# Rotary embedding of q and k in a decoder-trunk kernel: exchanging a head's halves by SBUF-to-SBUF transfers in place of a permutation product

## Chip, cores and metric

One core of one Trainium2 chip runs the whole kernel in one launch. The metric is the device time of that launch in microseconds, the median of several executions. TensorE is called PE in the profile, VectorE DVE, ScalarE ACT, GpSimd POOL and SyncE SP.

## What is computed

Two layers of a hybrid decoder trunk for 512 prompt tokens and 8 decode tokens, 520 columns in all. Each layer projects the normalised input to four mixers and their gates. The part that matters here is the attention's q and k, eight query heads and two key heads of 64 channels:

```python
def rope(x, pos):
    half = HEAD_DIM // 2
    ...
    x1, x2 = xf[..., :half], xf[..., half:]
    return jnp.concatenate([x1 * cos - x2 * sin, x2 * cos + x1 * sin], axis=-1).astype(x.dtype)

q = rope(rms_norm(aq.reshape(B, L, N_HEADS, HEAD_DIM), q_norm), pos)
k = rope(rms_norm(ak.reshape(B, L, N_KV_HEADS, HEAD_DIM), k_norm), pos)
```

Beside it runs mixer B, a depthwise convolution of width 31 over 512 channels (4 chunks of 128). Attention, the other mixers, the merge and a SwiGLU follow.

## The kernel before

Channels lie on the 128 partitions and tokens along a row, so everything is a chunk of 128 x 520 numbers. Every dense product is made exact enough by splitting each operand into a rounded part and its rest (`whi`, `wlo` for a weight tile, `xhi`, `xlo` for the input): three products for each of 8 input chunks, each in two halves of 260 columns, so 48 matmuls for an output chunk.

The list `SLOTS` is the order of the mixing stage: **slot** n is output chunk n, and all engines walk that list. Slots 0 to 7 give the wide convolution's inputs, 8 to 11 the four chunks of q (two heads each), 12 k, 13 v, and 14 to 25 the short convolution. In each slot, TensorE does the 48 matmuls (L604) and then its `side(n)`; VectorE does its `side(n)`, the weight rest two slots ahead (L1271, `lo`), the transfer of the chunk out of PSUM times rstd (L1262, `evac`), and some taps of the wide convolution (L1265, the table `TAPS_AT`: four in slots 8 and 9, two in slots 10 to 17); ScalarE does its `side(n)`, the rounding of a weight tile three slots ahead (L967, `hi`), and squares or sigmoids. Weight tiles come from DRAM on SP's queue (L579), two tiles to a load of 1 MB, into a ring of two loads. There are two PSUM buffers for output chunks, so slot n on TensorE needs slot n-2 taken out by VectorE.

GpSimd computes the fourth chunk of the wide convolution beside all this: 30 times a product `ssum <- cfu * weight` (L1728, TENSOR_SCALAR) and an addition `cacc <- cacc + ssum` (L1731, TENSOR_TENSOR), each waiting for the one before.

q and k go through these steps, chunk c = 0 to 4 (four of q, then k). ScalarE squares the chunk; TensorE sums over a head by a product with a block matrix of ones (L637, slot 9+c); ScalarE makes the factor by a logarithm and an exponential, `gt[:, 1]` (L950, slot 10+c); VectorE multiplies the chunk by gain and factor (L1265 `q<-q,pr,gt`, slot 10+c, semaphore `qk_n`); TensorE multiplies the result by the permutation matrix `rot`, which exchanges the two halves of each head and negates one, into PSUM banks 2 and 3 (L648, slot 11+c, `qk_r`); VectorE, in slot 12+c, multiplies those banks by the sine into `gt[:, 2]` (L1262 `gt<-m,cs`, `qk_rot`), the chunk by the cosine (L1262 `q<-q,cs`), and adds the two (L1262 `q<-q,gt`, `qk_out`). For c = 4 the names read `kt` in place of `q`. In slot 17 VectorE copies the decode tokens' columns to `kts` and `qz`, and TensorE's `side(17)` waits for those before its scores (L663).

```python
r1 = tt(halves(gt[:, 2]), m_halves(2), halves(sinm), ALU.mult, "qk_rot")
r2 = tt(v, v, cosm, ALU.mult)
st.need(r1, r2)
tt(v, v, gt[:, 2], ALU.add, "qk_out")
```

Of the kernel before, what the change touches and what calls it, by code (L numbers as in the profile page):

```python
# [27 lines left out]
ALU = mybir.AluOpType  # L28
# [3 lines left out]
P = 128  # L32
# [4 lines left out]
T = SEQ + NS  # L37
TH = T // 2
# [3 lines left out]
HEAD = 64  # L42
GROUP = 4
# [58 lines left out]
S_AQ, S_AV, S_SCH, S_GATE_A, S_GA, S_GATE_B = (FIRST[k] for k in ("aq", "av", "sch", ("gate", 0), "ga", ("gate", 1)))  # L102
# [75 lines left out]
NPAR = _at  # L178
CST = {}
_at = 0  # L180
for _name, _w in (("cos", T), ("sin", T), ("amask", 2 * P), ("ident", P), ("ones", P), ("ones64", P), ("rot", P),
                  ("eye8", NS)):
    CST[_name] = (_at, _at + _w)
    _at += _w
# [3 lines left out]
def constants():  # L188

    c = np.zeros((P, NCST), np.float32)  # L190
    half = HEAD // 2
    inv = np.float32(10000.0) ** (-np.arange(half, dtype=np.float32) / np.float32(half))
    pos = np.concatenate([np.arange(SEQ), np.full(NS, 2048)]).astype(np.float32)
    ang = (pos[:, None] * inv[None, :]).astype(np.float32)
    ang = np.tile(ang.T, (4, 1))
    q = np.arange(P)

    def put(name, v):
        a, b = CST[name]
        c[:v.shape[0], a:b] = v  # L200
    put("cos", np.cos(ang))
    put("sin", np.sin(ang))
    key = np.arange(2 * P)
    put("amask", np.where((key[None, :] > q[:, None]) & (key[None, :] <= q[:, None] + P), 0.0, NEG))
    put("ident", np.eye(P))
    put("ones", np.ones((P, P)))
    put("ones64", (q[:, None] // HEAD == q[None, :] // HEAD).astype(np.float32))
    rot = np.zeros((P, P))
    for m in range(P):
        if m % HEAD < half:  # L210
            rot[m + half, m] = -1.0
        else:
            rot[m - half, m] = 1.0
    put("rot", rot)
    put("eye8", np.eye(NS))
    s, t = q[:, None], q[None, :]
    glam = ((s // CHUNK == t // CHUNK) & (s <= t)).astype(np.uint32)
    tt = np.arange(T)
    scanm = np.tile(((tt % CHUNK != 0) & (tt < SEQ)).astype(np.float32), (P, 1))
    return c, glam, scanm  # L220


def build(nc, wt, xt, gm, par, cst, glam_d, scan_d, kc, vc, scst, ccst, gst,
          yt, o_sc, o_scs, o_cc, o_ccs, o_k, o_ks, o_v, o_vs, o_g, o_gs):
    ctx = ExitStack()
    with ctx:
# [44 lines left out]
        q = place("q", [P, GROUP, T], offset=base)  # L271
        kt = place("kt", [P, T], offset=base + 4 * SL)
# [26 lines left out]
        gt = place("gt", [P, 4, T])  # L299
# [13 lines left out]
        def cst_(name, rows=P):  # L313
            a, b = CST[name]
            return cs[0:rows, a:b]
# [4 lines left out]
        cosm, sinm, ident, ones = cst_("cos"), cst_("sin"), cst_("ident"), cst_("ones")  # L320
# [3 lines left out]
        m4 = ctx.enter_context(nc.psum_tensor("m4", [P, 4, 512], F32))  # L324
# [7 lines left out]
        def halves(ap):  # L332
            return ap.rearrange("p (a n) -> p a n", a=2)

        def m_halves(b):
            return m4[:, b:b + 2, 0:TH]
# [9 lines left out]
        def sem(name):  # L346
# [55 lines left out]
            "qk_ln": "their logarithm: the banks are read",  # L402
            "qk_rn": "the factor",
            "qk_n": "normalised chunk",
            "qk_r": "its rotated half, in banks 2 and 3",
            "qk_rot": "... times the sine: the banks are read",
            "qk_out": "rotated chunk",
            "v_t": "v transposed, in banks 0 and 1",
            "v_copied": "... in SBUF",
# [80 lines left out]
        s = {n: sem(n) for n in signals}  # L490
# [78 lines left out]
        with nc.Fori(0, DEPTH) as layer:  # L569
            with nc.Block() as block:  # L570
# [28 lines left out]
                def _(pe):  # L599
# [22 lines left out]
                    def side(n):  # L622
# [5 lines left out]
                        c = n - (S_AQ + 1)  # L628
                        if 0 <= c < 5:
# [6 lines left out]
                            for h in range(2):  # L636
                                ins = nc.tensor.matmul(m4[:, h, 0:TH], cst_("ones64"), gt[:, 0, h * TH:h * TH + TH],  # L637
                                                       start=True, stop=True)
                            ins.then_inc(s["qk_ss"], 1)
                        c = n - (S_AQ + 3)  # L640
                        if 0 <= c < 5:

                            pe.wait_ge(s["qk_n"], c + 1)
                            if c >= 1:
                                pe.wait_ge(s["qk_rot"], c)
                            src = q[:, c] if c < GROUP else kt[:]
                            for h in range(2):
                                ins = nc.tensor.matmul(m4[:, 2 + h, 0:TH], cst_("rot"), src[:, h * TH:h * TH + TH],  # L648
                                                       start=True, stop=True)
                            ins.then_inc(s["qk_r"], 1)  # L650
                        if n == S_AV + 3:

                            pe.wait_ge(s["acc_out"], S_AV + 1)
# [4 lines left out]
                        if n == SATT:  # L658
# [3 lines left out]
                            for b in range(NS):  # L662
                                ins = nc.tensor.matmul(m4[0:NQ, 0, 0:P], flat(qz)[:, b * NQ:b * NQ + NQ], kts[:, b],  # L663
                                                       start=b == 0, stop=b == NS - 1)
# [6 lines left out]
                        if n == SATT + 3:  # L671
# [3 lines left out]
                            for b in range(NS):  # L675
                                ins = nc.tensor.matmul(m4[:, 3, b * NS:b * NS + NS], vs[:, b], pts[:, b],
                                                       start=True, stop=True)
# [67 lines left out]
                        if n == G_U:  # L745
# [3 lines left out]
                            for c in range(NCHUNK):  # L749
                                r = slice((c % 2) * CHUNK, (c % 2) * CHUNK + CHUNK)  # L750
                                for h in range(4):
# [4 lines left out]
                                        start=True, stop=True)  # L756
# [189 lines left out]
                def _(a):  # L946
# [27 lines left out]
                    def rsqrt(out, in_, scale, eps, first, last):  # L974

                        st.need(act(out, in_, ACT.Ln, first, scale=scale, bias=eps))
                        act(out.rearrange("p a n -> p (a n)"), out.rearrange("p a n -> p (a n)"), ACT.Exp, last,
                            scale=-0.5)
# [17 lines left out]
                    def side(n):  # L996
# [14 lines left out]
                        if 0 <= c < 5:  # L1011
                            a.wait_ge(s["qk_ss"], c + 1)
                            if c:
                                a.wait_ge(s["qk_n"], c)
                            rsqrt(halves(gt[:, 1]), m_halves(0), 1.0 / HEAD, RMS_EPS, "qk_ln", "qk_rn")
                        if n == SATT:
                            a.wait_ge(s["v_t"], 1)
                            act(vb[:].rearrange("p b n -> p (b n)"), m4[:, 0], name="act_order")
                            st.need(act(vnew, m4[0:NS, 1, 0:P], name="v_copied"))
                            a.wait_ge(s["vs_in"], 16)  # L1020
                            for b in range(NS):
                                load(vs[WIN - 1:WIN, b], vnew[b:b + 1], "vnew_in")
# [235 lines left out]
                def _(dve):  # L1258
                    st = Steps(dve, "vec_order")

                    def tt(out, in0, in1, op, name=None):
                        return st(nc.vector.tensor_tensor(out, in0, in1, op), name)  # L1262
# [45 lines left out]
                    def side(n):  # L1308
# [11 lines left out]
                        if 0 <= c < 5:  # L1320

                            v = q[:, c] if c < GROUP else kt[:]
                            dve.wait_ge(s["qk_r"], c + 1)
                            if c:
                                st.need(("qk_out", c))
                            r1 = tt(halves(gt[:, 2]), m_halves(2), halves(sinm), ALU.mult, "qk_rot")
                            r2 = tt(v, v, cosm, ALU.mult)
                            st.need(r1, r2)
                            tt(v, v, gt[:, 2], ALU.add, "qk_out")
# [573 lines left out]
```

## Time and profile before

| | us |
|---|---|
| median of 3 runs (2064.05 to 2064.55) | 2064.53 |
| the profiled execution | 2065.61 |
| its span, first to last instruction | 2063.8 |

| engine | busy us | share of the span |
|---|---|---|
| TensorE matmul | 2012.2 | 97% |
| TensorE weight load | 1971.5 | 96% |
| VectorE | 1226.2 | 59% |
| ScalarE | 781.8 | 38% |
| GpSimd | 380.7 | 18% |

The profile describes one execution, so its rows add up to its own time, which is 1.1 us above the median. Busy TensorE time is modelled from the starts of the matmuls and doesn't tell by itself which engine is waited for; the waits and the timeline of a stretch do. Both layers run the same program, the second one 1024 us after the first. In the rows, "out<-in" are the program's buffers: `m` is the four-bank PSUM tensor `m4`, `acc` the output chunks in PSUM, `cs` the constants (cosine, sine, matrices), `pr` the parameters; all other names are in SBUF.

### The profile page before, as it was taken

The numbers are of one execution on the slowest core, as the hardware profiler recorded it, in microseconds if no ns is written. First come the engines' busy times: TensorE is split into PE (matmuls) and PEld (weight loads), VectorE is DVE, ScalarE is ACT, GpSimd is POOL, SyncE is SP. The second block draws the span as 40 slices with busy tenths as digits, with TensorE's granted clock in tenths as the row PEclk, the third lists the DMA queues.
The fourth block names the chain that finished last, engine by engine and source line by source line (L and its number), as shares of the span: only waits on it lengthen the run. The fifth ranks groups of instructions, "written<-read, shape, count | busy, mean of one in ns | idle before, by whom it ended". The sixth has DMA issues, their size and how long they took to land.

```text
span 2063.8 us, 39007 instructions
## 1 busy us (share of the span) xinstructions
PE 2012.2 (97%) x16572; PEld 1971.5 (96%) x16572; DVE 1226.2 (59%) x1667; ACT 781.8 (38%) x1209; POOL 380.7 (18%) x238
## 2 busy tenths in 40 slices
PE   6999999999999999999989999999999999999998
PEld 6999999999999999999989999999999999999998
DVE  4898668755556543355539985787455454533445
ACT  4323533553543332233233144336534334322332
POOL 0695000311103000000307940002111130000003
PEclk9999999999999999999999999999999999999999
DMA  7524522222322222222444243222223222232223
GB/s 239 98 85 83 83 77 98 83 95 83 124 82 103 82 97 92 97 82 79 141 121 80 101 63 82 93 83 87 91 82 141 86 92 92 82 101 85 99 77 128
DMA packets 70041, 199.57 MB, mean 97 GB/s; under 512 B 41555, under 2 KB 42707, under 8 KB 51409
## 3 DMA queue, kind: packets, MB, share of 16 engines
q1 hardware_dynamic: 26144, 177.50, 26.1%
q10 hardware_dynamic: 43760, 20.11, 5.7%
q8 instruction: 104, 1.70, 0.4%
q14 instruction: 33, 0.26, 0.0%
HBM read 187.42 MB, written 12.29 MB: 97 GB/s over the span
## 4 chain that ended last, share of the span: by engine, by line
PE 42%; DVE 6%; issue 1%; ACT 1%; POOL 0%; ACTq 0%; DVEq 0%; POOLq 0%
PE acc L604 40%; DVE cacc L1265 1%; DVE wlo L1271 1%; DVE q L1262 1%; DVE sct L1265 0%; ACT tmp L950 0%; PE m L701 0%; PE m L688 0%; PE m L714 0%; PE m L618 0%; DVE gt L1262 0%; DVE small L1262 0%; PE m L816 0%; PE m L788 0%; PE m L826 0%
## 5 line engine op out<-in xcount | busy, mean ns | idle before, releaser
L604 PE MATMUL acc<-xhi,wlo 128*128 128x260 f32 x3680 | 754.1, 286 | 28.7 <-PEq L567 19.4
L604 PE MATMUL acc<-xhi,whi 128*128 128x260 f32 x3680 | 743.0, 284 | 0.0
L604 PE MATMUL acc<-xlo,whi 128*128 128x260 f32 x3680 | 742.4, 283 | 0.0
L604 PEld LDWEIGHTS acc<-xhi,wlo 128*128 128x128 f32 x3680 | 571.0, 189 | 42.3 <-issue 34.6
L604 PEld LDWEIGHTS acc<-xhi,whi 128*128 128x128 f32 x3680 | 569.3, 189 | 0.0
L604 PEld LDWEIGHTS acc<-xlo,whi 128*128 128x128 f32 x3680 | 569.0, 189 | 0.0
L1271 DVE TENSOR_TENSOR wlo<-raw,whi 128x1024 fp32r<-128x1024 f32 (+3 forms) x344 | 435.7, 1275 | 36.7 <-ACT whi L967 35.3
L967 ACT ACTIVATE whi<-raw 128x1024 fp32r<-128x1024 f32 (+3 forms) x344 | 332.1, 994 | 252.7 <-PE acc L604 195.2
L950 ACT ACTIVATE gt<-gt 128x520 f32<-128x520 f32 x226 | 144.4, 639 | 214.1 <-DVE gt L1262 209.2
L1262 DVE TENSOR_TENSOR gt<-acc,rstd 128x520 f32<-128x520 f32 x80 | 55.9, 699 | 210.6 <-PE acc L604 185.6
L604 PE MATMUL acc<-hhi,whi 128*128 128x260 f32 x704 | 141.5, 282 | 0.0
L604 PE MATMUL acc<-hlo,whi 128*128 128x260 f32 x704 | 141.5, 282 | 0.0
L604 PE MATMUL acc<-hhi,wlo 128*128 128x260 f32 x704 | 141.4, 282 | 0.0
L1265 DVE SCALAR_TENSOR_TENSOR cacc<-cfu,pr,cacc 128x512 f32<-128x512 f32 x180 | 140.1, 804 | 1.6
L1772 POOL TENSOR_TENSOR tmp<-x 128x520 f32<-128x520 f32 x2 | 2.1, 1054 | 656.0 <-DVE x L1691 656.0
L1728 POOL TENSOR_SCALAR ssum<-cfu,pr 128x512 f32<-128x512 f32 x60 | 120.9, 2016 | 5.9
L1659 DVE TENSOR_TENSOR gt<-acc,rstd 128x520 f32<-128x520 f32 x44 | 30.8, 700 | 134.0 <-PE acc L604 122.8
L604 PEld LDWEIGHTS acc<-hlo,whi 128*128 128x128 f32 x704 | 108.4, 188 | 0.0
L604 PEld LDWEIGHTS acc<-hhi,wlo 128*128 128x128 f32 x704 | 108.3, 188 | 0.0
L604 PEld LDWEIGHTS acc<-hhi,whi 128*128 128x128 f32 x704 | 108.3, 188 | 0.0
L604 PE MATMUL acc<-ohi,wlo 128*128 128x260 f32 x512 | 106.7, 290 | 0.5 <-DVE gt L1262 0.5
L604 PE MATMUL acc<-ohi,whi 128*128 128x260 f32 x512 | 103.0, 283 | 0.0
(224 smaller groups left out, 2093.8 us busy)
## 6 DMA issues: line engine op xcount, KB each, us to landing
raw<-in_wt SPq DMA_DIRECT2D x142, 1024.0 KB, 4.8
raw<-in_wt SPq DMA_DIRECT2D x16, 768.0 KB, 4.3
raw<-in_wt SPq DMA_DIRECT2D x16, 640.0 KB, 3.8
x<-yt ACTq DMA_DIRECT2D x2, 2080.0 KB, 9.4
yt<-x ACTq DMA_DIRECT2D x16, 260.0 KB, 2.1
x<-in_xt SPq DMA_DIRECT2D x4, 520.0 KB, 5.0
yt<-in_xt SPq DMA_DIRECT2D x1, 2080.0 KB, 16.3
s<-in_gs ACTq DMA_DIRECT2D x4, 512.0 KB, 3.8
```

The costliest lines, as they stand in the source:

```text
L604: ins = nc.tensor.matmul(out[:, h], a, b[:, h * TH:h * TH + TH], start=first and n == 0, stop=last and n == 2)
L950: return st(nc.scalar.activation(out, in_, func, **kw), name)
L967: nc.scalar.activation(whi[:, ts, 0:length], raw[:, e, off:off + length], ACT.Copy)\
L1262: return st(nc.vector.tensor_tensor(out, in0, in1, op), name)
L1265: return st(nc.vector.scalar_tensor_tensor(out=out, in0=in0, scalar=scalar, in1=in1, op0=op0, op1=op1), name)
L1271: nc.vector.tensor_tensor(wlo[:, ts, 0:length], raw[:, e, off:off + length], whi[:, ts, 0:length].bitcast(F32), ALU.subtract)\
L1659: nc.vector.tensor_tensor(halves(t), acc_of(0), halves(rstd[:]), ALU.mult)\
L1728: st(nc.gpsimd.tensor_scalar(ssum[:, 0:SEQ], cfu[:, c, w:w + SEQ], par_("cc", c * W2 + w), None, ALU.mult))
L1772: nc.gpsimd.tensor_tensor(tmp[:, 0], x[:, 0], x[:, 0], ALU.mult).then_inc(s["ss_sq"], 1)
```

## The change

The matrix `rot` and TensorE's products with it (L648) are gone. In their place ScalarE, in its `side` of slot 11+c after the logarithm and exponential, waits for `qk_n` c+1 and, from the second chunk on, for `qk_rot` c, and issues four transfers on its own DMA queue, each 32 partitions x 520 numbers from SBUF to SBUF: the halves exchanged, into `gt[:, 3]`. The sign is put into the sine. VectorE waits for the four transfers (16 counts each) and multiplies `gt[:, 3]` by the sine. The constants that are loaded at the start get 128 columns narrower.

```diff
-    put("sin", np.sin(ang))
+    first = (np.arange(P) % HEAD < half)[:, None]
+    put("sin", np.where(first, -np.sin(ang), np.sin(ang)))
...
-                        c = n - (S_AQ + 3)
-                        if 0 <= c < 5:
-
-                            pe.wait_ge(s["qk_n"], c + 1)
-                            if c >= 1:
-                                pe.wait_ge(s["qk_rot"], c)
-                            src = q[:, c] if c < GROUP else kt[:]
-                            for h in range(2):
-                                ins = nc.tensor.matmul(m4[:, 2 + h, 0:TH], cst_("rot"), src[:, h * TH:h * TH + TH],
-                                                       start=True, stop=True)
-                            ins.then_inc(s["qk_r"], 1)
...
+                        c = n - (S_AQ + 3)
+                        if 0 <= c < 5:
+
+                            a.wait_ge(s["qk_n"], c + 1)
+                            if c:
+                                a.wait_ge(s["qk_rot"], c)
+                            for p0 in range(0, P, HEAD // 2):
+                                p1 = p0 ^ (HEAD // 2)
+                                src = q[p1:p1 + HEAD // 2, c] if c < GROUP else kt[p1:p1 + HEAD // 2]
+                                load(gt[p0:p0 + HEAD // 2, 3], src, "qk_r")
...
-                            dve.wait_ge(s["qk_r"], c + 1)
+                            dve.wait_ge(s["qk_r"], 64 * (c + 1))
...
-                            r1 = tt(halves(gt[:, 2]), m_halves(2), halves(sinm), ALU.mult, "qk_rot")
+                            r1 = tt(gt[:, 2], gt[:, 3], sinm, ALU.mult, "qk_rot")
```

ScalarE's program around slot 12 before (`gt<-q` is the square, the next two the factor, `whi` the rounded weight tile; in brackets the semaphores waited for):

```order
L950 ACTIVATE gt<-q 128x520 [waits qk_ss,acc_out]
L950 ACTIVATE gt<-m 128x520 [waits qk_n,qk_ss]
L950 ACTIVATE gt<-gt 128x520 [waits qk_ln]
L967 ACTIVATE whi<-raw 128x1024 [waits acc_done]
L950 ACTIVATE gt<-kt 128x520 [waits qk_ss,acc_out]
```

And now (its lines are numbered 17 lower):

```order
L933 ACTIVATE gt<-q 128x520 [waits qk_ss,acc_out]
L933 ACTIVATE gt<-m 128x520 [waits qk_n,qk_ss]
L933 ACTIVATE gt<-gt 128x520 [waits qk_ln]
L936 DMA gt<-q 32x520 [waits qk_rot,qk_n]
L936 DMA gt<-q 32x520 x3
L950 ACTIVATE whi<-raw 128x1024 [waits acc_done]
L933 ACTIVATE gt<-kt 128x520 [waits qk_ss,acc_out]
```

Four DMA issues and a wait for VectorE's `qk_rot` stand between the factor and the weight tile's rounding.

VectorE's program around slot 13 before:

```order
L1262 TENSOR_TENSOR kt<-acc,rstd 128x520 [waits acc_done]
L1265 SCALAR_TENSOR_TENSOR cacc<-cfu,pr,cacc 128x512 [waits vec_order] x2
L1262 TENSOR_TENSOR gt<-m,cs 128x520 [waits qk_out,qk_r]
L1262 TENSOR_TENSOR q<-q,cs 128x520
L1262 TENSOR_TENSOR q<-q,gt 128x520 [waits vec_order,qk_rot]
```

And now (its lines are numbered 7 lower):

```order
L1255 TENSOR_TENSOR kt<-acc,rstd 128x520 [waits acc_done]
L1258 SCALAR_TENSOR_TENSOR cacc<-cfu,pr,cacc 128x512 [waits vec_order] x2
L1255 TENSOR_TENSOR gt<-gt,cs 128x520 [waits qk_out,qk_r]
L1255 TENSOR_TENSOR q<-q,cs 128x520
L1255 TENSOR_TENSOR q<-q,gt 128x520 [waits vec_order,qk_rot]
```

The number and order of VectorE's instructions is the same; the first input of the product with the sine is `gt` in place of `m`.

## Rows read from the trace of the kernel before

**Rows 1.** The page's first part: engine, busy us, share, instructions.

```profile
PE 2012.2 (97%) x16572; PEld 1971.5 (96%) x16572; DVE 1226.2 (59%) x1667; ACT 781.8 (38%) x1209; POOL 380.7 (18%) x238
```

**Rows 2.** Busy time by stretch, slots 9 to 19 of layer 0 (stretch, length, engines, clock).

```profile
80.00:160.00 80.00, 76.21 (x588) 74.25 (x587) 75.80 (x95) 21.80 (x32) 76.20 (x42) 0.98 0.31 95
```

**Rows 3.** Waits of PE, 93 to 139 us: us in total, times, longest.

```profile
PE m L663 <- DVE qz L1342: 3.6, 1, 3.6
```

**Rows 4.** Timeline of DVE, slots 12 and 13: start us, us, engine, line.

```profile
101.07 0.69 DVE L1262 TENSOR_TENSOR kt<-acc,rstd 128x520 f32<-128x520 f32 x1
101.68 1.40 DVE L1265 SCALAR_TENSOR_TENSOR cacc<-cfu,pr,cacc 128x512 f32<-128x512 f32 x2
103.00 0.69 DVE L1262 TENSOR_TENSOR gt<-m,cs 128x520 f32<-128x520 f32 x1
103.61 1.19 DVE L1262 TENSOR_TENSOR q<-q,cs 128x520 f32<-128x520 f32 x1
104.90 1.00 DVE L1262 TENSOR_TENSOR q<-q,gt 128x520 f32<-128x520 f32 x1
105.83 0.75 DVE L1265 SCALAR_TENSOR_TENSOR q<-q,pr,gt 128x520 f32<-128x520 f32 x1
106.50 2.31 DVE L1271 TENSOR_TENSOR wlo<-raw,whi 128x1024 fp32r<-128x1024 f32 x1
108.73 0.69 DVE L1262 TENSOR_TENSOR vt<-acc,rstd 128x520 f32<-128x520 f32 x1
```

**Rows 5.** Timeline of POOL beside it.

```profile
100.16 2.42 POOL L1728 TENSOR_SCALAR ssum<-cfu,pr 128x512 f32<-128x512 f32 x1
102.66 1.58 POOL L1731 TENSOR_TENSOR cacc<-cacc,ssum 128x512 f32<-128x512 f32 x1
104.34 1.89 POOL L1728 TENSOR_SCALAR ssum<-cfu,pr 128x512 f32<-128x512 f32 x1
106.31 1.41 POOL L1731 TENSOR_TENSOR cacc<-cacc,ssum 128x512 f32<-128x512 f32 x1
```

**Rows 6.** Instructions on gt, 60 to 130 us: duration ns min/median/max, starts.

```profile
L1262 DVE TENSOR_TENSOR gt<-m,cs x5: 685/686/687, 95.3 to 125.1; 128x520 f32<-128x520 f32 x5
L1262 DVE TENSOR_TENSOR cfu<-gt x2: 686/686/687, 63.3 to 69.0; 128x512 f32<-128x512 f32 x2
```

**Rows 7.** All instructions of L1728 and of L1731: duration ns min/median/max.

```profile
L1728 POOL TENSOR_SCALAR ssum<-cfu,pr x60: 1562/1893/2952, 73.4 to 1205.9; 128x512 f32<-128x512 f32 x60
L1731 POOL TENSOR_TENSOR cacc<-cacc,ssum x60: 1265/1496/2301, 75.1 to 1207.5; 128x512 f32<-128x512 f32 x60
```

**Rows 8.** Timeline of PE at the end of slot 12.

```profile
100.33 1.04 PE L637 MATMUL m<-gt,cs 128*128 128x260 f32 x4
101.20 1.04 PE L648 MATMUL m<-q,cs 128*128 128x260 f32 x4
101.89 0.60 PE L604 MATMUL acc<-xhi,wlo 128*128 128x260 f32 x2
```

**Rows 9.** Timelines: ACT's factor and rounding, the first product, DMA issues.

```profile
90.50 0.64 ACT L950 ACTIVATE gt<-gt 128x520 f32<-128x520 f32 x1
91.04 1.04 ACT L967 ACTIVATE whi<-raw 128x1024 fp32r<-128x1024 f32 x1
95.33 0.69 DVE L1262 TENSOR_TENSOR gt<-m,cs 128x520 f32<-128x520 f32 x1
93.66 29.22 SPq L579 DMA_DIRECT2D raw<-in_wt  x3
130.09 5.14 ACTq L953 DMA_DIRECT2D vs<-tmp  x8
```

**Rows 10.** DMA issues: count, KB each, median us from issue to landing.

```profile
raw<-in_wt SPq DMA_DIRECT2D x142, 1024.0 KB, 4.8
vs<-tmp ACTq DMA_DIRECT2D x16, 0.5 KB, 1.7
```

**Rows 11.** Busy time by stretch around the wait of rows 3 (the 0.50 is PE's clock).

```profile
139.00:140.00 1.00, 1.00 (x7) 1.00 (x6) 1.00 (x1) 0.00 (x0) 0.92 (x2) 0.50 0.00 0
```

More of the change, by code:

```diff
@@ L180 @@
 _at = 0
-for _name, _w in (("cos", T), ("sin", T), ("amask", 2 * P), ("ident", P), ("ones", P), ("ones64", P), ("rot", P),
+for _name, _w in (("cos", T), ("sin", T), ("amask", 2 * P), ("ident", P), ("ones", P), ("ones64", P),
                   ("eye8", NS)):
@@ L207, in constants @@
     put("ones64", (q[:, None] // HEAD == q[None, :] // HEAD).astype(np.float32))
[L208 to L214, printed above, removed]
     put("eye8", np.eye(NS))
@@ L404, in build @@
             "qk_n": "normalised chunk",
-            "qk_r": "its rotated half, in banks 2 and 3",
-            "qk_rot": "... times the sine: the banks are read",
+            "qk_r": "its halves exchanged, by DMA",
+            "qk_rot": "... times the sine, which has the sign",
             "qk_out": "rotated chunk",
```

## The prediction
> **What bounds the kernel now.** I read the page first: TensorE is busy for 97% of the span and VectorE for 59% [rows 1], which makes a product taken from TensorE look like time won. That is a mean over stages, so I went to the stretch that the change touches. From 80 to 160 us of layer 0, slots 9 to 19, VectorE is busy for 75.80 of 80 us and GpSimd for 76.20 [rows 2]; both are full there, and TensorE's 76.21 says little, since its busy time is modelled. Next, who waits for whom: between 93 and 139 us VectorE has no wait on another engine at all, and TensorE has one, 3.6 us at the end, when it stands before its scores until VectorE has copied `qz` [rows 3]. So in these slots the chain runs through VectorE, and whatever TensorE loses or gains before that wait is made up in it.
>
> Then VectorE slot by slot. One slot takes 7.66 us (`kt<-acc` at 101.07 to `vt<-acc` at 108.73) with no gap [rows 4]. TensorE's own slot is not much shorter: 48 matmuls, the sum over a head and the product with the permutation, which begins at 101.20 and gives way at 101.89, 0.69 us [rows 8].
>
> What stretches VectorE's slot? The product with the sine from PSUM takes 685 to 687 ns in all five instances [rows 6], though GpSimd is in the middle of something each time. The next one, `q<-q,cs`, has the same size but both inputs in SBUF, and takes 1.19 us [rows 4]; a product of two SBUF inputs before GpSimd has begun took 0.686 (`cfu<-gt`) [rows 6]. Beside GpSimd's starts [rows 5] this reads as a turn-taking. The 0.69 us of work in `q<-q,cs` would begin at 104.11 if it ends at 104.80, and GpSimd's addition ends at 104.24. `wlo<-raw,whi` lasts 2.31 us and ends at 108.81; its own 1.21 us would begin at 107.60, and the addition beside it ends at 107.72. So a VectorE instruction with two SBUF inputs stands until GpSimd's addition is within 0.12 us of its end, and GpSimd in turn stands until VectorE's has let go. The addition that began at 102.66 had to let the tap end at 103.08 and held VectorE off until 104.11, some 1.1 us. GpSimd's product with a weight holds for less: the addition `q<-q,gt` at 104.90 was stretched by 0.31 us to 1.00, hence about 0.5 us after `q<-q,cs` let go, and the pair of taps at 101.68 was not stretched at all (1.40 us for two) though such a product ran until 102.58. In one slot VectorE stands for 0.50 + 0.31 + 1.10 = 1.91 us.
>
> **The change, part by part.**
>
> *Products with the permutation.* Ten chunks in two layers, 0.69 us of TensorE each, up to 0.87 if the change of matrices after it is counted like that after the sum over a head [rows 8]: 6.9 to 8.7 us of TensorE. I cost this at nothing. It lies beside VectorE's slot; TensorE reaches its scores earlier and waits there longer than 3.6 us [rows 3].
>
> *The product with the sine.* Its own length stays 0.69 us, but its first input moves from PSUM to SBUF, and it becomes one of the instructions that take turns with GpSimd. In the slot shown it begins at 103.00, just when GpSimd's addition gets its turn, and that addition did 0.69 of its 1.1 us under it for free. Now VectorE stands: the product would end at 104.80 instead of 103.69, `q<-q,cs` no longer stands behind that addition (0.50 us back), but GpSimd's next product gets in between. Below, it costs nothing, if GpSimd's turns slide under other free work (the 0.69 us of `kt<-acc`, or the part of its product in which it holds nobody off). Above, each of the ten loses 1.11 us, 104.11 less 103.00, and nothing is given back: 11.1 us. I take the middle that follows from GpSimd's work being fixed: it has 30 such pairs a layer whatever VectorE does, and each product takes 0.69 us away in which it ran for free, so 10 x 0.69 = 6.9 us. It is nearest to the row because the addition filled that window wholly.
>
> The Trainium skill (SBUF — State Buffer, section "Who interferes with whom") speaks against the change by a rule of its own: a VectorE instruction with two SBUF inputs contends with a GpSimd instruction that reads SBUF, and whichever starts first keeps the shared port for the whole instruction. The rows agree for GpSimd's addition and not for its product, beside which two taps ran unstretched; by the page the sum would be that of the fourth rival below.
>
> *The transfers.* ScalarE issues eight transfers of 0.5 KB in 5.14 us, 0.64 us each [rows 9], so four cost it 2.6 us a chunk. Its slot holds that beside a weight tile of 1.04 us and three instructions of about the factor's 0.64 [rows 9], in all 5.6 of 7.66 us, so ScalarE keeps up. Behind them on its engine stand the weight tile's rounding, due one VectorE slot later, and the next square, due in the same slot; both come about 2.6 us later and are still early. On its queue nothing else is issued between the convolution's states in slot 8 and slot 17. A small transfer from SBUF to SBUF lands 1.7 us after issue; a load of 1 MB takes 4.8 [rows 10]. From one product with the sine to the next: 0.69 + 2.6 + 1.7 = 5.0 us, under a slot's 7.66, so chunks 1 to 4 are covered by the rest of VectorE's slot, with 2.7 us to spare. Chunk 0 is tight. Its factor is out at 91.14, four issues end at 93.7, landing at about 95.4, and VectorE wants it at 95.33 [rows 9]. A weight load starts at 93.66, so it may land as late as such a load, 4.8 us after issue, at 98.5. Bounds: 0 to 3.2 us a layer; I take 0.5, near the small transfer's row, so 1.0 us in two layers.
>
> *Constants 128 columns narrower, the sign in the sine:* nothing; the load stands before the first slot among loads of several MB.
>
> Sum, against the profiled execution: 2065.6 + 0 + 6.9 + 1.0 = 2073.5. Its time is 1.1 us above the median of the runs, so the forecast is **2072.4 us**, 7.9 us or 0.4% slower. A measurement of this kernel can tell about 0.2%, 4.1 us, from no change.
>
> **The rivals.**
>
> 1. *GpSimd moves aside.* Its turns fall under VectorE's remaining free work, or it ends its 30 pairs earlier and gives later slots back what it took. For: its product holds nobody off for about two thirds of its length. Against: GpSimd is busy for 76.20 of 80 us [rows 2], and in the row its addition uses the whole window. 0 to 3 us: about 2066.5, no change.
> 2. *TensorE was the bound after all,* and what it is spared shows. For: 97% [rows 1], and its slot is within a few tenths of VectorE's. Against: VectorE has no gap and TensorE ends in a wait of 3.6 us. It would decide only if VectorE's stretched instructions hid a wait for TensorE. 6.9 to 8.7 us less: 2056 to 2057.6, faster.
> 3. *The transfers are late.* If they land as slowly as a weight load, 4.8 us, the loop is 0.69 + 2.6 + 4.8 = 8.1 us, 0.4 over VectorE's slot for eight chunks, 3 us, and chunk 0 costs 2.7 us more than I took, in two layers 5. On top of the forecast: 2080. Against: the small transfers run on rings that the weight loads use for less than half of each two slots.
> 4. *GpSimd's product holds for its whole length too.* The product with the sine would then stand behind 1.56 us [rows 7] instead of a part of 1.1: 10 x 1.56 = 15.6 us, 2080. Against: the two taps at 101.68.
> 5. *TensorE's clock.* After its wait of 3.6 us the granted clock was 0.50, 1.2 GHz [rows 11]. Shorter slots on TensorE and longer ones on VectorE leave it waits of about 1.7 us in each of five slots; if these lower the clock too, its 48 matmuls take up to twice 5.8 us and it becomes the bound: some 3 us more than the forecast in each layer if half of that shows, 2078.
>
> **How the numbers follow.** Forecast 0.55, rival 1 0.18, rival 2 0.06, rival 3 0.10, rival 4 0.07, rival 5 0.04. The predicted time is the forecast's. The range runs from 2064.5 (the lower bound, nothing) to 2080.5: the upper bound of 11.1 us and a late chunk 0 (5 us) give 2080.6, and rivals 3 to 5 lie within. Left out are rival 2 and perhaps half of rivals 3 and 4, under 2 in 10. Faster by over 0.2%: rival 2, 0.06. Within 0.2%: rival 1, 0.18. Slower: the rest, 0.76.
>
> **What would show it.** In the changed profile: `gt<-gt,cs` longer than 0.69 us in several instances, up to 1.8, where `gt<-m,cs` was 0.69 in all; VectorE without waits between slots 12 and 17 except one before the first of them, under 1 us; TensorE's wait for `qz` several us longer than 3.6; four issues of 0.6 us a chunk on ScalarE's queue and no VectorE wait for ScalarE's weight tile. A `gt<-gt,cs` of 0.69 throughout with no later time would be rival 1; VectorE waits on the transfers in every chunk, rival 3; TensorE at 0.50 within slots 12 to 16, rival 5. A time under 2060 would make the reading of the bound wrong.

## The result, and the profile after

The changed kernel takes 2070.32 us (median of 9 runs, 2067.47 to 2072.84), the kernel before 2064.55 beside it (9 runs, 2063.89 to 2066.09). The ratio is 1.0028, with a 95% interval of 1.0018 to 1.0038: 5.8 us slower, between 3.7 and 7.8. The forecast was 7.9 us slower. The profiled execution took 2071.61 us, its span 2068.5. Its times are set against those of the profile before in two layers, so a difference in one place stands for two.

The page's first part, after, stands beside [rows 1]:

```profile
PE 2005.3 (97%) x16532; PEld 1965.3 (95%) x16532; DVE 1229.8 (59%) x1667; ACT 781.7 (38%) x1209; POOL 386.2 (19%) x238
```

TensorE lost 40 matmuls and 6.9 us of busy time, and nothing of that shows in the time. VectorE and GpSimd, with the same number of instructions as before, are busy for 3.6 and 5.5 us longer. Where VectorE's go is seen in its timeline of the same slot as [rows 4] (start us, us, engine, line):

```profile
101.99 0.69 DVE L1255 TENSOR_TENSOR kt<-acc,rstd 128x520 f32<-128x520 f32 x1
102.60 1.40 DVE L1258 SCALAR_TENSOR_TENSOR cacc<-cfu,pr,cacc 128x512 f32<-128x512 f32 x2
103.92 1.78 DVE L1255 TENSOR_TENSOR gt<-gt,cs 128x520 f32<-128x520 f32 x1
105.63 0.69 DVE L1255 TENSOR_TENSOR q<-q,cs 128x520 f32<-128x520 f32 x1
106.42 0.92 DVE L1255 TENSOR_TENSOR q<-q,gt 128x520 f32<-128x520 f32 x1
107.26 0.75 DVE L1258 SCALAR_TENSOR_TENSOR q<-q,pr,gt 128x520 f32<-128x520 f32 x1
107.93 2.32 DVE L1264 TENSOR_TENSOR wlo<-raw,whi 128x1024 fp32r<-128x1024 f32 x1
110.17 0.69 DVE L1255 TENSOR_TENSOR vt<-acc,rstd 128x520 f32<-128x520 f32 x1
```

And GpSimd's beside it, to be read with [rows 5]:

```profile
103.58 1.57 POOL L1724 TENSOR_TENSOR cacc<-cacc,ssum 128x512 f32<-128x512 f32 x1
105.24 2.42 POOL L1721 TENSOR_SCALAR ssum<-cfu,pr 128x512 f32<-128x512 f32 x1
107.75 1.42 POOL L1724 TENSOR_TENSOR cacc<-cacc,ssum 128x512 f32<-128x512 f32 x1
```

The slot is 8.18 us long (101.99 to 110.17) where it was 7.66. The product with the sine takes 1.78 us instead of 0.69: with both inputs in SBUF it stands behind the addition that GpSimd began at 103.58. But `q<-q,cs`, which stood 0.50 us behind that addition before, now follows in 0.69, and `q<-q,gt` is 0.08 shorter: 1.09 - 0.50 - 0.08 = 0.51, and 0.52 by the slot's length, within rounding. GpSimd's next product, ready when the addition ended at 105.15, does not get between the two: it takes 2.42 us, where 1.56 is its least [rows 7]. That fits a wait until the second of VectorE's is nearly done: its 1.56 us would begin at 106.10 (107.66 less 1.56), and `q<-q,cs` ends at 106.32.

The instances of the product, 60 to 131 us (duration ns min/median/max, first and last start):

```profile
L1255 DVE TENSOR_TENSOR gt<-gt,cs x5: 687/1783/1784, 95.8 to 127.6; 128x520 f32<-128x520 f32 x5
```

Four of five are long. The fifth, in slot 16, takes 0.69; there `kt<-kt,cs` is the long one, as it was before. TensorE's wait before its scores, 3.6 us in [rows 3], has become (us in total, times, longest):

```profile
PE m L646 <- DVE qz L1335: 9.5, 1, 9.5
```

It gives back what TensorE was spared, and VectorE's delay comes on top. Behind this wait TensorE's granted clock stayed at 0.50 (1.2 GHz) for longer. The next two rows show the same stretch of its work, 3.4 to 5.4 us after its scores began (stretch, its length, PE's busy time, clock, DMA share, GB/s). Before:

```profile
142.00:144.00 2.00, 2.00 (x16) 0.92 0.97 389
```

and after:

```profile
144.46:146.46 2.00, 2.00 (x10) 0.53 0.96 389
```

So TensorE did 10 matmuls there instead of 16, and came later to its next meeting with VectorE, the product with `sprob`. Before, it stood waiting for `sprob`:

```profile
138.61 3.44 PE L663 MATMUL m<-kts,qz 128*64 128x128 f32 x16 [3.59 <-DVE qz L1342]
153.50 0.40 PE L604 MATMUL acc<-xhi,whi 128*128 128x260 f32 x2
154.10 0.27 PE L669 MATMUL m<-cs,sprob 64*128 64x64 f32 x1 [0.20 <-DVE sprob L1357]
```

After, it needed 15.71 us instead of 14.89 from the start of the scores to the last pair of matmuls ahead of that product:

```profile
141.09 3.67 PE L646 MATMUL m<-kts,qz 128*64 128x128 f32 x16 [9.54 <-DVE qz L1335]
156.80 0.40 PE L598 MATMUL acc<-xhi,whi 128*128 128x260 f32 x2
157.28 0.27 PE L652 MATMUL m<-cs,sprob 64*128 64x64 f32 x1
```

The transfers are as cheap as hoped here. The issue of chunk 0's and chunk 1's, the landing, and an issue further on that nobody had asked about, on ScalarE's queue:

```profile
90.92 3.13 ACTq L936 DMA_DIRECT2D gt<-q  x4
97.62 2.44 ACTq L936 DMA_DIRECT2D gt<-q  x4
152.16 1.12 ACTq L936 DMA_DIRECT2D o_v<-vt  x1
```

```profile
gt<-q ACTq DMA_DIRECT2D x32, 65.0 KB, 2.0
```

VectorE has no wait for any of them; the first product begins at 95.75, right behind its predecessor. The last issue, the write of v to memory after the decode tokens' softmax, took 0.37 us in both layers before, 1.12 and 0.93 now. Behind it on ScalarE stands the rounding of branch A's chunk, for which VectorE waited 1.33 us before:

```profile
155.93 0.72 DVE L1255 TENSOR_TENSOR olo<-sct,ohi 128x520 fp32r<-128x520 f32 x1 [2.08 <-ACT ohi L933]
```

So two places lose time. The first is known, VectorE's product. The second, TensorE and ScalarE both late for what follows the scores, was not foreseen.

### The profile page after: what moved, and what is told of

Read it like the earlier page. It is cut to its first block, busy times and chain, and to the rows that moved or that the text cites. A ratio compares the mean times of both kernels' runs of the same rounds, so it can differ in the third digit from the quotient of the medians.

```text
span 2068.5 us, 38967 instructions
## 1 busy us (share of the span) xinstructions
PE 2005.3 (97%) x16532; PEld 1965.3 (95%) x16532; DVE 1229.8 (59%) x1667; ACT 781.7 (38%) x1209; POOL 386.2 (19%) x238
## 4 chain that ended last, share of the span: by engine, by line
PE 43%; DVE 5%; issue 1%; ACT 1%; POOL 0%; DVEq 0%; POOLq 0%
PE acc L598 40%; DVE cacc L1258 1%; DVE wlo L1264 1%; DVE gt L1255 0%; DVE q L1255 0%; ACT tmp L933 0%; PE m L684 0%; PE m L671 0%; PE m L697 0%; PE m L612 0%; DVE sct L1258 0%; PE m L799 0%; PE m L771 0%; PE m L809 0%; PE m L646 0%
```

## The experiments

Two stretches of each profile separate the two places. Stretch A runs from the arrival of k's chunk (`kt<-acc`, slot 12) to the first copy of `qz`; stretch B from ScalarE's `sprob` exponential to its first `prob` one. T is TensorE's part of what leads into B: from the start of its scores to the last pair of matmuls ahead of its product with `sprob`. Between stretches A and B, from the copy of `qz` to `sprob`, 10.75 to 10.79 us passed in every kernel and layer of this table. All values are us, worked out from starts in the timelines, layer 0 / layer 1.

| kernel | A | B | T | issue of `o_v` | time against before (95%) |
|---|---|---|---|---|---|
| before | 37.10 / 37.09 | 16.10 / 16.09 | 14.89 / 14.88 | 0.37 / 0.37 | |
| the change | 38.66 / 38.66 | 16.81 / 16.81 | 15.71 / 15.87 | 1.12 / 0.93 | 1.0028 (1.0018 to 1.0038) |
| e1: product from SBUF alone | 38.69 / 38.69 | 16.32 / 16.19 | 15.61 / 15.51 | 0.37 / 0.37 | 1.0023 (1.0013 to 1.0032) |
| e2: product back in PSUM | 37.09 / 37.09 | 16.09 / 16.92 | 14.79 / 15.38 | 0.37 / 0.61 | 1.0014 (1.0005 to 1.0023) |
| e5: sine in PSUM | 37.08 / 37.10 | 16.09 / 16.93 | 15.19 / 15.12 | 0.37 / 0.62 | 1.0013 (1.0004 to 1.0022) |
| e7: transfers alone, unread | 37.10 / 37.13 | 16.09 / 16.08 | 14.86 / 14.91 | 0.37 / 0.37 | 0.9999 (0.9990 to 1.0008) |
| e9: neither products nor transfers | 37.08 / 37.09 | 16.89 / 16.80 | 15.72 / 15.65 | 1.23 / 0.80 | 1.0011 (1.0001 to 1.0020) |
| e10: products, and transfers waited for | 37.10 / 37.12 | 16.42 / 16.10 | 15.71 / 14.93 | 0.37 / 0.37 | 0.9999 (0.9990 to 1.0008) |

**e1, the product's source alone.** The kernel before, TensorE's product kept, its result unread:

```diff
-                            r1 = tt(halves(gt[:, 2]), m_halves(2), halves(sinm), ALU.mult, "qk_rot")
+                            r1 = tt(gt[:, 2], gt[:, 3], sinm, ALU.mult, "qk_rot")
```

> The kernel before, with one change: VectorE's product with the sine reads gt[:, 3] in SBUF (old contents, so the rotation is left out of q and k) in place of the PSUM banks. TensorE's product with the permutation and all waits stay; there are no transfers. Theory A (the product, with two SBUF inputs, now takes turns with GpSimd): four of five products a layer stretch to about 1.78 us, the copy of qz comes 2.0 us later in each layer, the whole about 4.1 us slower than before, 2068.6. Theory B (the transfers and their issue on ScalarE cost the time): no change from before, within 1 us, and all products at 0.69 us.

Measured: 2068.07 us, ratio 1.0023. The instances of the product, 60 to 131 us:

```profile
L1262 DVE TENSOR_TENSOR gt<-gt,cs x5: 689/1784/1797, 95.2 to 127.0; 128x520 f32<-128x520 f32 x5
```

Same lengths and the same stretch A as in the change, within 0.03 us, without one transfer. The lengthening belongs to the place of the product's input.

**e2, the rest of the change.** The change with its product reading PSUM, which a longer sum over the head in chunk 0 fills:

```diff
-                            r1 = tt(gt[:, 2], gt[:, 3], sinm, ALU.mult, "qk_rot")
+                            r1 = tt(halves(gt[:, 2]), m_halves(2), halves(sinm), ALU.mult, "qk_rot")
```

> The changed kernel, with all its transfers, issues and waits, but VectorE's product with the sine reads PSUM banks 2 and 3 (filled once a layer by the head sum of chunk 0, so the rotation is left out). Theory A: the product is 0.69 us again, the copy of qz no later than before; what is left over the kernel before is at most the late DMA issue behind it on ScalarE, 0.7 us a layer, so 2064.5 to 2066.0. Theory B: still about 5.8 us slower than before, 2070.

Measured: 2067.75 us, ratio 1.0014. Stretch A is that of the kernel before, so the product's part is gone; but about 2.9 us stay, more than the 1.5 that theory A allowed. Half of it is the edit's own. In slot 11 VectorE waits for TensorE, which does more in chunk 0, and the two taps behind take 2.45 us instead of 1.40:

```profile
94.11 0.70 DVE L1255 TENSOR_TENSOR q<-acc,rstd 128x520 f32<-128x520 f32 x1 [0.47 <-PE acc L598]
94.73 2.45 DVE L1258 SCALAR_TENSOR_TENSOR cacc<-cfu,pr,cacc 128x512 f32<-128x512 f32 x2
```

From the `wlo` ahead of this to `kt<-acc`, VectorE takes 9.53 us instead of the 8.80 of the kernel before, and as much longer in layer 1: 1.5 us in two layers.

**e3, GpSimd idle.** In both kernels, 29 of GpSimd's 30 pairs are left out:

```diff
-                    for w in range(1, W2):
+                    for w in range(1, 2):
```

> The kernel before with 29 of GpSimd's 30 pairs of the wide convolution left out (its fourth chunk is not computed). It is the yardstick for the next run. VectorE's slot loses its 1.9 us of standing; both theories expect it faster than before by several us a layer, TensorE being the bound of slots 9 to 16, about 2050 to 2060.

> The changed kernel with 29 of GpSimd's 30 pairs left out. Theory A: with nobody to take turns with, all products are 0.69 us, and TensorE's saved 0.69 us in each of ten slots shows: 3 to 7 us faster than the kernel before with the same pairs left out. Theory B: slower than that kernel by 1.4 to 5.8 us, since the transfers remain.

Measured: 2049.79 us (ratio 0.9935, 0.9921 to 0.9948) and 2040.55 us (0.9886, 0.9871 to 0.9901). The change is then 9.2 us faster, more than expected and a little over the price of TensorE's products (6.9 to 8.7 us). VectorE's timeline of the change, slot 12 to 13:

```profile
100.42 0.70 DVE L1255 TENSOR_TENSOR kt<-acc,rstd 128x520 f32<-128x520 f32 x1 [0.79 <-PE acc L598]
...
102.36 0.69 DVE L1255 TENSOR_TENSOR gt<-gt,cs 128x520 f32<-128x520 f32 x1
...
107.07 0.70 DVE L1255 TENSOR_TENSOR vt<-acc,rstd 128x520 f32<-128x520 f32 x1 [0.79 <-PE acc L598]
```

The same product from SBUF takes 0.69 us where GpSimd rests. VectorE now waits 0.79 us a slot for TensorE, and in the kernel before with the same pairs left out 1.6:

```profile
100.59 0.70 DVE L1262 TENSOR_TENSOR kt<-acc,rstd 128x520 f32<-128x520 f32 x1 [1.63 <-PE acc L604]
108.09 0.70 DVE L1262 TENSOR_TENSOR vt<-acc,rstd 128x520 f32<-128x520 f32 x1 [1.66 <-PE acc L604]
```

The slot is 6.65 us long in the change (100.42 to 107.07) and 7.50 in its partner, so in these slots each matmul saved is time saved. It is not that TensorE's part was cheap; it was covered.

**e4, room on VectorE with GpSimd at work.** In both kernels, VectorE's 16 taps of slots 10 to 17 move to slots 24 to 29:

```diff
-for _first, _last, _m in ((4, 7, 3), (8, 9, 4), (10, 17, 2), (20, 21, 2), (29, 29, 2), (30, 33, 1), (34, 37, 2),
-                          (38, 41, 1), (42, 53, 3)):
+for _first, _last, _m in ((4, 7, 3), (8, 9, 4), (20, 21, 2), (24, 25, 1), (26, 26, 2), (27, 27, 4), (28, 28, 6),
+                          (29, 29, 3), (30, 33, 1), (34, 37, 2), (38, 41, 1), (42, 53, 3)):
```

> The kernel before with the 16 convolution taps of slots 10 to 17 moved to slots 24 to 29, where VectorE waits for TensorE (complete computation). If VectorE is the bound of slots 10 to 17 (theory A), its slot falls from 7.66 to about 6.3 us, below TensorE's, its copy of qz comes earlier, and TensorE's wait of 3.6 us for it shrinks or goes: 4 to 8 us faster than before, about 2058. If TensorE was the bound there, no change.

> The changed kernel with the same 16 taps moved (complete computation). Theory A: VectorE's slot has room again, though its product still takes turns with GpSimd; TensorE's slot is 0.69 us shorter, so it should come out at or below the kernel before with moved taps, 0 to 6 us below it, about 2055. Theory B (the transfers themselves cost the time): slower than that kernel by 1.4 to 5.8 us.

Measured: the kernel before 2063.55 us (ratio 0.9990, 0.9981 to 0.9999), the change 2059.39 (0.9974, 0.9965 to 0.9983). The kernel before gains less than expected. Part of the reason is that TensorE is next: VectorE now stands for TensorE's permutation, and its slot is still 7.50 us long (`kt<-acc` at 101.00, `vt<-acc` at 108.50):

```profile
110.26 0.70 DVE L1262 TENSOR_TENSOR gt<-m,cs 128x520 f32<-128x520 f32 x1 [1.05 <-PE m L648]
```

The other part lies later. VectorE begins with `sprob` 4.1 us earlier than before in layer 0 (143.36 for 147.47), but at 218 us, with the first of the moved taps behind it, 0.3 us of that are left (`gt<-acc` at 218.27 for 218.59). What takes the gain back there wasn't followed.

The change takes off the permutation that is waited for, and is 4.2 us faster than its partner and faster than the kernel before. The sign of this change is set by which engine is full in these slots.

**e5 and e6, the sine in PSUM.** What e2 stayed above the kernel before asked for a cleaner form: ScalarE copies the sine into the free banks 2 and 3 once a layer, so the product again has one input in PSUM.

```diff
+                            if c == 0:
+                                act(m_halves(2), halves(sinm), name="sin_in")
...
-                            r1 = tt(gt[:, 2], gt[:, 3], sinm, ALU.mult, "qk_rot")
+                            if c == 0:
+                                dve.wait_ge(s["sin_in"], 1)
+                            r1 = tt(halves(gt[:, 2]), halves(gt[:, 3]), m_halves(2), ALU.mult, "qk_rot")
```

> The changed kernel, with one copy on ScalarE a layer that puts the sine into banks 2 and 3 of PSUM ahead of the first product; the product then reads one input from SBUF and one from PSUM. Theory A (the product with two SBUF inputs takes turns with GpSimd; in the two traces that is 1.57 us a layer from the first k product to the copy of q, and 0.5 us for the product before): the product is back at 0.69 us in every slot, the copy of q comes some 2 us a layer earlier, and the time is 3.3 to 4.5 us below the changed kernel's 2070.3, that is 2065.8 to 2067.0. What stays above the kernel before (1 to 2.5 us) is then the transfers'. Rival B (the cost is the transfers': their issue on ScalarE, their landing): the product is short, but the time stays at 2069 to 2071. Rival C (any VectorE product beside GpSimd's products is delayed, wherever its inputs lie): the product stays at 1.78 us and the time at 2070 to 2071.

Measured: 2067.76 us, ratio 1.0013; 2.6 us below the change by medians, a little less than theory A gave. The instances, 60 to 131 us:

```profile
L1258 DVE TENSOR_TENSOR gt<-gt,m x5: 681/684/695, 95.8 to 125.4; 128x520 f32<-128x520 f32 x5
```

All are short again, and chunk 1's `q<-q,cs` takes 1.18, as before (1.19). The Trainium skill (SBUF — State Buffer, section "Who interferes with whom") says that a VectorE instruction with at most one SBUF input, outside the two-port performance modes, does not contend with GpSimd; these five agree, at 0.68 to 0.70 us. Rival C falls. e6 is the same with e4's taps.

> The changed kernel with the sine in PSUM, and with VectorE's 16 taps of slots 10 to 17 moved to slots 24 to 29. With the taps moved and both inputs in SBUF the time was 2059.4, and three of five products a layer took 1.18 to 1.38 us there instead of 0.69. Theory A: these 0.5 to 0.7 us go, so 1.5 to 3.5 us less, 2056 to 2058. Rival: with the taps gone VectorE is not what TensorE waits for in those slots, the product is covered, and the time stays within 1 us of 2059.4.

Measured: 2058.22 us (5 runs, 2055.47 to 2062.52; ratio 0.9962, 0.9948 to 0.9976). It lies 1.2 us below e4's version, less than theory A gave, and the two intervals overlap. Either version beats both kernels; that e6 beats e4's is not shown.

**e7 and e10, do the transfers cost anything?** e7 adds them to the kernel before, unread and copied from the sine's table; e10 lets them copy q and k as in the change, and VectorE wait for each, while it goes on reading TensorE's result:

```diff
+                                src = q[p1:p1 + HEAD // 2, c] if c < GROUP else kt[p1:p1 + HEAD // 2]
+                                load(gt[p0:p0 + HEAD // 2, 3], src, "qx")
...
                             dve.wait_ge(s["qk_r"], c + 1)
+                            dve.wait_ge(s["qx"], 64 * (c + 1))
```

> The kernel before, whose products with the permutation matrix stay, and beside them the 20 transfers a layer from ScalarE's queue at the places of the change; they copy a part of the sine's table into a tile that nobody reads, and no engine but ScalarE waits for them. Theory A (VectorE's product carries the cost, the transfers nearly nothing): 0 to 1 us above the kernel before. Rival B (the transfers have a price of their own: 10 us a layer of ScalarE's queue, and after them a slower issue of the write of v, 0.37 us before and 0.93 to 1.12 us after the change, with ScalarE's rounding behind it): 1.5 to 3.5 us above, and that issue over 0.5 us in at least one of the layers. If TensorE's products matter too, they would show here as nothing, since they stay.

> The kernel before with its products on TensorE and the product with the sine from PSUM, and beside them the change's transfers of the halves of q and k; VectorE waits for each of them, but reads TensorE's result. Theory L1 (what stays of the difference comes with TensorE's products gone): within 0.7 us of the kernel before. Theory L2 (VectorE's or ScalarE's waits for the transfers): 1.5 to 3 us above. Theory L3 (no rest): within 1 us; L1 and L3 part on the other run of this call. In each case the write of v is issued in 0.37 us if its slow issues come only where TensorE's products are gone.

Measured: 2064.80 us beside 2065.36, and 2065.47 beside 2065.68; both ratios 0.9999 (0.9990 to 1.0008). Twenty transfers a layer, issued, landed and waited for, cost nothing that can be measured beside a VectorE that is full. Where it has room, it does wait for them. With the taps moved, chunk 0's transfers came late in one layer of each profile, in e4's change in layer 1, in e6 in layer 0:

```profile
1117.37 1.34 DVE L1255 TENSOR_TENSOR gt<-gt,cs 128x520 f32<-128x520 f32 x1 [4.37 <-DMA gt<-q]
100.03 0.70 DVE L1258 TENSOR_TENSOR gt<-gt,m 128x520 f32<-128x520 f32 x1 [5.04 <-DMA gt<-q]
```

In the other layers VectorE waited 1.29 and 1.28 us for them; e8 below has a wait of 5.00 us too. What these waits cost wasn't tested; the execution of e6 with 5.04 us was the slowest of its five.

**e9, neither products nor transfers.** e5 without the four `load` lines and without VectorE's wait for them.

> The run with the sine in PSUM, without the 20 transfers a layer and the waits for them: the exchange of the halves is left out, and the product reads a tile that nobody fills. It has neither TensorE's products nor the transfers. The run with the sine in PSUM stood at 1.0013 (1.0004 to 1.0022) of the kernel before, 2.7 us above it, and the one with TensorE's products and unread transfers at 0.9999. Theory L1 (the rest comes with TensorE's products gone: it waits for the copy of q 7.8 us instead of 3.6 and works at a lower clock longer after it): 1.5 to 3 us above the kernel before. Theory L2 (the rest comes from waiting for the transfers): within 0.7 us of it. Theory L3 (there is no such rest beyond the scatter of the runs): within 1 us.

Measured: 2067.57 us beside 2065.68, ratio 1.0011 (1.0001 to 1.0020): about as much as e5, without a transfer. This speaks for theory L1, that the rest comes with TensorE's products gone, and against L2, the transfers. Its size by the runs is loose, 0.2 to 4.1 us, so the runs alone don't exclude L3. The traces show the place, stretch B, and two causes in it.

The first is TensorE's lower clock behind its longer wait for `qz`, as theory L1 had it. In the change and in e9, T is 0.8 to 1.0 us longer than before. Between the copy of `qz` and `sprob` this costs nothing, since VectorE sets the pace there; but TensorE comes late to its product with `sprob`. In e1, and in e10's layer 0, this can be seen alone, since `o_v` was issued in 0.37 us: T is 0.6 to 0.8 us longer, and B 0.1 to 0.3 us. In e10's layer 0 TensorE doesn't wait for `sprob`:

```profile
140.31 3.67 PE L664 MATMUL m<-kts,qz 128*64 128x128 f32 x16 [3.60 <-DVE qz L1355]
156.02 0.40 PE L605 MATMUL acc<-xhi,whi 128*128 128x260 f32 x2
156.35 0.27 PE L670 MATMUL m<-cs,sprob 64*128 64x64 f32 x1
```

Its wait for `qz` was as long as before, 3.60 us, so the wait's length isn't all that decides how long the clock stays low.

The second is the slow issue of `o_v`, which delays ScalarE's rounding and with it VectorE's `sprob`. In layer 1 of e2 and of e5 it is what decides: `o_v` took 0.61 and 0.62 us, and VectorE's two short instructions behind it, `small<-small` and `sprob`, lasted 0.56 and 0.72 us instead of 0.14 and 0.34. TensorE, though its T is longer too, then waited for `sprob`, and B is 0.8 us longer. In e5's layer 1:

```profile
1179.61 0.27 PE L653 MATMUL m<-cs,sprob 64*128 64x64 f32 x1 [1.03 <-DVE sprob L1355]
```

In the change and in e9 both engines are late, and B is 0.7 to 0.8 us longer; how that splits is not shown.

In the profiles of six kernels that have TensorE's products, with transfers or without (before, e1, e7, e10, and e3's and e4's kernels before), the issue of `o_v` took 0.37 us in all twelve layers. In those of seven without the products (the change, e2, e5, e6, e9, and e3's and e4's changed kernels) it took 0.51 to 2.08 in nine layers of fourteen, and 0.37 in the other five. A longer wait of TensorE is not the reason: the 2.08 us came in e3's changed kernel, where TensorE didn't wait for `qz` at all. All seven are made from the change, so its narrower constants and its other program go with the missing products; which of these matters is open.

**e8, the writes elsewhere.** e6, with the four writes of keys and values moved from ScalarE's queue to the one that loads the weights, ahead of unit 16 of the layer:

```diff
-                    units(4, T_F2A // 2, 2048)
+                    units(4, U_KV, 2048)
...
+                        sp.dma_start(d[bass.ds(layer, 1)].rearrange(f"z {names} -> (z a) {' '.join('bcdef'[:n - 2])}"),
+                                     src).then_inc(s["kv_out"], 16)
+                    units(U_KV, T_F2A // 2, 2048)
```

> As the run with the sine in PSUM and the taps later, and the four writes of the keys and values to memory (k, v and the decode tokens' two) are issued from the queue that loads the weights, between two weight loads, instead of ScalarE's. ScalarE's four issues there took 1.5 to 2.2 us, with the rounding of branch A's chunk behind them, for which VectorE waited 1.3 to 2.1 us. If that wait is on the path, 1 to 1.5 us a layer go: 2 to 3 us less than without this edit. If TensorE has work of its own meanwhile, the wait only moves: within 0.8 us of it. If the weight loads come late behind the writes, it is slower, by 1 us or more.

Measured: 2062.54 us (ratio 0.9988, 0.9979 to 0.9997), 4.3 us slower than e6. Slower was one of the cases; whether late weight loads are the reason wasn't followed.

## Why the prediction was right, and where its terms were not

The sign, the engine and the mechanism held: slower, on VectorE, by a product that takes turns with GpSimd. The sum came within 2.1 us, but partly by luck: a term too large made up for one left out.

- **What bounds the stretch**: right. With VectorE full, TensorE's spared time turned into a wait for `qz`, 9.5 us for 3.6. e3 and e4 show the other side: as soon as VectorE has room, the same edit gains 9.2 and 4.2 us.
- **The product with the sine, 10 x 0.69 = 6.9 us**: right mechanism, too large. The traces show 0.50 for the first product, in slot 12 ahead of `kt<-acc`, and 1.57 for the four after it (stretch A): 2.07 us a layer, 4.1 in all. The failed step is "GpSimd's next product gets in between": VectorE ran the product with the sine and `q<-q,cs` one behind the other, and GpSimd's product waited for both. So `q<-q,cs` kept the 0.50 us it had back, and four products of a layer paid 0.52 each. The one in slot 16 paid nothing. e1 has this part alone: 4.7 us by its ratio (2.7 to 6.6).
- **Products with the permutation at nothing**: wrong. They saved nothing, but taking them away had a cost that I had not looked for: 0.71 and 0.72 us a layer in stretch B of the change, 1.4 in all, 2.3 and 2.7 by the ratios of e9 and e5 (each about 2 us either way). TensorE's wait for `qz`, costed at nothing, brought a lower clock behind it, and the write of v was issued slowly; the first is shown, why the second happens is open. 4.1 + 1.4 = 5.5 us, beside the 5.8 measured. The two profiled spans differ by only 4.7 us (2068.5 and 2063.8): at places that the edit doesn't touch an execution can lose or regain more than a microsecond, as between 1249 and 1525 us of the kernel before, where the change's `gt<-acc` goes from 6.3 to 4.7 us late. So the closeness of 5.5 to 5.8 is partly luck too.
- **Transfers, 1.0 us**: nothing. Chunk 0's four issues took 3.13 us instead of 2.6 and still landed in time. The median transfer of 65 KB lands in 2.0 us, near the chosen row's 1.7. That they landed in time was not sure: with the taps moved VectorE waited 4.4 to 5.0 us for chunk 0's, more than the bound of 3.2 us a layer.
- **Rival 1** (GpSimd moves aside): right for one product in five. **Rival 2** (TensorE the bound): refuted here, and what happens in e3. **Rival 3** (late transfers): refuted here, no wait; it is seen for single chunks in e4, e6 and e8. **Rival 4** (GpSimd's product holds for its whole length): refuted; two taps beside it still take 1.40 us. **Rival 5** (the clock within slots 12 to 16): refuted as put; from 93 to 136 us the clock was 1.00. It was lower for longer only through the wait before the scores and behind it, and there it is a part of stretch B's 0.7 us.

## What to carry to other kernels

Before work is moved off an engine, look in that very stretch for the engine that is full; what is saved on its neighbour is nothing, and a new home for an operand (PSUM to SBUF) can put a full engine's instruction into turns with GpSimd. Count such turns for the pair of neighbouring instructions, since what one of them loses the next may get back. When an edit fails, ask whether the full engine can be emptied first: with 16 taps moved out of these slots, the same edit became the gain.

## What the runs showed of the hardware that was not expected

- VectorE's back-to-back instructions keep GpSimd out: its waiting product took 2.42 us rather than 1.56 at its least, beside two VectorE products with two SBUF inputs, one behind the other.
- Four transfers of 32 partitions cost ScalarE's queue 2.44 us to issue, 0.61 each (for chunk 0 up to 3.13 in the change and 3.53 in e8), against 0.34 to 0.42 for a write of 128 partitions. The 65 KB land 2.0 us after issue by the median of the change, but VectorE waited up to 5.04 us for them in e6.
- The issue of one write took 0.51 to 2.08 us instead of 0.37, only in kernels made from the change, without TensorE's ten products; also in e9, where the exchange's transfers were left out.
- After waits of the same length, 3.60 and 3.56 us, TensorE's clock was low for longer in one layer of e10 than in the other: T is 15.71 us in layer 0 and 14.93 in layer 1.
